# Scan of a gated delta rule on one core: the chunk's inverse as T(1+A)(1+A²), summed in PSUM

## The reference, cut to what matters

```python
def step(S, inp):
    w_t, k_t, v_t, kk_t, a_t = inp[:5]
    s_kk = jnp.einsum('nbhvk,nbhk->nbhv', S, kk_t)
    S = S * w_t[..., None, :] - s_kk[..., :, None] * (kk_t * a_t)[..., None, :] + v_t[..., :, None] * k_t[..., None, :]
    y_t = jnp.einsum('nbhvk,nbhk->nbhv', S, inp[5]) if emit else None
    return S, y_t
```

## Time and profile before

| | |
|---|---|
| runs | 5050.57, 5038.10, 5045.04 us; median 5045.04 |
| profiled execution | 5050.79 us, its span 5049.0 us |
| granted TensorE clock, mean over the span | 0.975 |
| PE matmul busy | 4816.4 us (95%), 27502 records |
| DVE, ACT, POOL busy | 1475.1, 1053.9, 321.6 us |
| the scan's steady rounds | from 3000.66 to 3421.77 us of the span |

### The profile page before, as it was taken

One profiled execution on the slowest core, in us unless ns is written; L12 is line 12 of the kernel. 1 busy time (PEld: TensorE's weight loads), 2 busy tenths in 40 slices (PEclk: granted clock), 3 DMA queues, 4 the chain that ended last, 5 costly groups with the idle time before them and its releaser, 6 DMA issues.

```text
span 5049.0 us, 63120 instructions
## 1 busy us (share of the span) xinstructions
PE 4816.4 (95%) x27502; PEld 2642.5 (52%) x27502; DVE 1475.1 (29%) x2777; ACT 1053.9 (21%) x2046; POOL 321.6 (6%) x302
## 2 busy tenths in 40 slices
PE   8999999999999999999998989998999999899999
PEld 4444444444444445665554568786444555544444
DVE  3621110462121010000324347775102444310100
ACT  1131000123100022110214124443112333311210
POOL 1100000110000000000014100000000010000000
PEclk9999999999999999999999999999999999899999
DMA  3151212125122211111134422223111000011211
GB/s 121 59 200 68 83 62 80 61 75 192 67 75 68 82 42 59 50 50 43 62 133 134 140 70 78 78 74 114 48 47 45 26 28 32 26 43 74 82 68 58
DMA packets 91841, 378.36 MB, mean 75 GB/s; under 512 B 7985, under 2 KB 33713, under 8 KB 62129
## 3 DMA queue, kind: packets, MB, share of 16 engines
q1 hardware_dynamic: 80608, 332.92, 18.7%
q0 software_dynamic: 9808, 37.75, 2.3%
q10 hardware_dynamic: 1152, 3.67, 0.2%
HBM read 334.46 MB, written 39.85 MB: 74 GB/s over the span
## 4 chain that ended last, share of the span: by engine, by line
PE 91%; DVE 4%; ACT 2%; issue 2%; DMA 0%; POOL 0%; POOLq 0%; SPq 0%; DVEq 0%; ACTq 0%
PE ps L521 43%; PE ps L333 23%; PE ps L542 7%; PE ps L3385 2%; PE ps L1781 2%; PE ps L339 1%; PE ps L3312 1%; PE ps L990 1%; PE ps L946 1%; PE ps L3396 1%; PE ps L2477 1%; PE ps L2428 1%; PE ps L3315 1%; PE ps L3311 1%; PE ps L3313 1%
## 5 line engine op out<-in xcount | busy, mean ns | idle before, releaser
L521 PE MATMUL ps<-A,W 128*128 128x512 f32 (+1 forms) x5408 | 2174.4, 562 | 24.5 <-DVE A L493 8.8
L521 PEld LDWEIGHTS ps<-A,W 128*128 128x128 f32 x5408 | 1028.5, 191 | 1118.9 <-issue 1076.0
L333 PE MATMUL ps<-A,W 64*64 64x64 f32 (+3 forms) x3264 | 664.5, 380 | 17.3 <-DMA W<-in_rw_in 6.1
L333 PEld LDWEIGHTS ps<-A,W 128*128 128x128 f32 (+2 forms) x3264 | 351.5, 162 | 309.7 <-issue 277.9
L333 PE MATMUL ps<-A 64*64 64x64 f32 (+3 forms) x8416 | 446.6, 238 | 63.3 <-ACT A L3538 23.2
L333 PEld LDWEIGHTS ps<-A 64*64 64x64 f32 (+2 forms) x8416 | 408.5, 148 | 166.7 <-issue 94.3
L542 PE MATMUL ps<-W,A 128*128 128x512 f32 (+1 forms) x896 | 367.6, 572 | 1.8 <-ACT A L1567 1.8
L542 PEld LDWEIGHTS ps<-W,A 128*128 128x128 f32 x896 | 173.1, 194 | 191.7 <-issue 183.6
L435 ACT ACTIVATE A<-R 128x512 f32<-128x512 f32 (+1 forms) x96 | 52.6, 574 | 782.7 <-DVE R L1577 354.6
L1697 DVE SCALAR_TENSOR_TENSOR A<-ps,V,A 128x512 f32<-128x512 f32 (+1 forms) x48 | 31.0, 661 | 486.9 <-PE ps L333 486.3
L1577 DVE SCALAR_TENSOR_TENSOR R<-ps,MOD,R 128x512 f32<-128x512 f32 (+1 forms) x48 | 31.7, 662 | 439.4 <-PE ps L521 438.1
(11 more groups left out here) (358 smaller groups left out, 4210.0 us busy)
## 6 DMA issues: line engine op xcount, KB each, us to landing
W<-in_ada SPq DMA_DIRECT2D x48, 1024.0 KB, 5.3
W<-in_w_up SPq DMA_DIRECT2D x44, 1024.0 KB, 4.8
W<-in_w_down SPq DMA_DIRECT2D x32, 704.0 KB, 4.0
W<-in_w_in SPq DMA_DIRECT2D x18, 1024.0 KB, 4.8
W<-in_sgu_v SPq DMA_DIRECT2D x16, 1024.0 KB, 4.9
W<-in_sgu_u SPq DMA_DIRECT2D x16, 1024.0 KB, 4.8
W<-in_sgu_z SPq DMA_DIRECT2D x16, 1024.0 KB, 4.9
W<-in_sgu_o SPq DMA_DIRECT2D x16, 1024.0 KB, 4.7
```

The costliest lines, as they stand in the source:

```text
L333: r = e.matmul(out, a, b, start=start and i == 0, stop=stop and i == len(pairs) - 1, skip_group_check=loose)
L521: t = e.matmul(ps, w[:, k, c:c + mc], x(k, seg), start=k == 0, stop=k == kt - 1)
```

## The change

The two rounds that add an identity give way to one square and one product that don't need each other. The first `series` makes A² = `nE`ᵀ`nEt` with no identity; the second makes T(1+A) (turned) from `Z1` and `T16`, also with no identity; ACT puts the first into `Z2` and the second over `nE`. `inverse` then sums 64 products in place of 32 into the same two banks: for each head T(1+A)·A² and T·(1+A). The number of banks taken, the order of the strands and the copies on ACT, DVE and POOL stay. DVE's wait before it overwrites `nE` moves from `Z3` to `Q` of the step before.

```diff
--- before.py
+++ after.py
@@ -2449,7 +2449,6 @@
 
     S_, b = pl.S, pl.scan
     AR, KA, KD, KB = b.AR[s % 3], b.KA[s % 2], b.KD[s % 2], b.KB[s % 2]
-    one = table(pl, "id64")
 
     def blocks(g):
         names = [(k, s, g, c) for k in ("Et", "E") for c in range(2)]
@@ -2472,27 +2471,26 @@
         e.wait_ge(*event)
         for x in names:
             e.wait_ge(*free(pl, x))
-        for c in range(2):
-            i = one[HALF[c], :].rearrange("p (o c) -> p o c", o=1).to_broadcast([64, 8, 64])
-            e.matmul(by_heads(ps[c][HALF[c], :]), one[HALF[c], :], i, start=True, stop=False, skip_group_check=True)
         for hh in range(8):
             for c in range(2):
                 t = product(e, ps[c][HALF[c], 64 * hh:64 * hh + 64],
-                            [(left[HALF[c], 8 * g + hh, :], right[HALF[c], 8 * g + hh, :])], start=False, loose=True)
+                            [(left[HALF[c], 8 * g + hh, :], right[HALF[c], 8 * g + hh, :])])
         t.then_inc(*S_.inverse_made.next((s, g, stage)))
 
     def inverse():
 
         names = [("Q", s, c) for c in range(2)]
         ps = [take(pl, x, "0123") for x in names]
-        e.wait_ge(*S_.act_blocks.at(s, 1, "Z3"))
+        e.wait_ge(*S_.act_blocks.at(s, 1, "TZ"))
         for x in names:
             e.wait_ge(*free(pl, x))
         for hh in range(8):
-            for g in range(2):
-                for c in range(2):
-                    t = product(e, ps[c][HALF[g], 64 * hh:64 * hh + 64],
-                                [(b.T16[HALF[c], 8 * g + hh, :], b.Z1[HALF[c], 8 * g + hh, :])])
+            for left, right in ((b.nE, b.Z2), (b.T16, b.Z1)):
+                for g in range(2):
+                    for c in range(2):
+                        t = product(e, ps[c][HALF[g], 64 * hh:64 * hh + 64],
+                                    [(left[HALF[c], 8 * g + hh, :], right[HALF[c], 8 * g + hh, :])],
+                                    start=hh == 0 and left is b.nE, stop=False, loose=True)
         t.then_inc(*S_.inverse_made.next((s, "Q")))
 
     def tokens(c):
@@ -2534,12 +2532,12 @@
     tokens(0)
     yield
     for g in range(2):
-        series(g, "Z2", b.nE, b.Z1, S_.pool_blocks.at(s, g))
+        series(g, "A2", b.nE, b.nEt, S_.dve_blocks.at(s, g, "E"))
         yield
     tokens(1)
     yield
     for g in range(2):
-        series(g, "Z3", b.nE, b.Z2, S_.act_blocks.at(s, g, "Z2"))
+        series(g, "TZ", b.Z1, b.T16, S_.pool_blocks.at(s, g))
         yield
     values(None)
     yield
@@ -2681,12 +2679,12 @@
     tokens(0)
     yield
     for g in range(2):
-        series(g, "Z2", b.Z2)
+        series(g, "A2", b.Z2)
         yield
     tokens(1)
     yield
     for g in range(2):
-        series(g, "Z3", b.Z1)
+        series(g, "TZ", b.nE)
         yield
     e.wait_ge(*S_.inverse_made.at(s, "Q"))
     if s >= 2:
@@ -2865,7 +2863,7 @@
     def blocks(g):
         e.wait_ge(*S_.inverse_made.at(s, g, "E"))
         if s and g == 0:
-            e.wait_ge(*S_.inverse_made.at(s - 1, 1, "Z3"))
+            e.wait_ge(*S_.inverse_made.at(s - 1, "Q"))
         for name, dst, mask in (("Et", b.nEt, later), ("E", b.nE, earlier)):
             for c in range(2):
                 at = (name, s, g, c)
```

## The result

| | before | changed |
|---|---|---|
| median of 20 runs each, us | 5050.31 (5038.10 to 5067.22) | 5037.47 (5023.59 to 5047.03) |
| ratio | | 0.9974, 95% interval 0.9966 to 0.9983 |
| profiled execution, span, us | 5049.0 | 5035.1 |
| scan, from the first decay product of its own to the first product of the output stage, us | 519.08 | 504.28 |
| nine steady rounds, us | 380.69 | 366.10 |

The change is faster by 0.26%, 13 us, with 9 to 17 inside the interval. 5037.47 lies in that range. The gain of 13 us lies between my own case (13 to 21, forecast 16.5) and the rival in which the supply takes more (10.5), and 0.26% falls into the outcome "within 0.3%", which I had given 0.41 against 0.54 for more.

What follows compares the result with a forecast made beforehand. Taken as bound: PE up to L, then DVE's chain. Ten rounds at 1.3 (13.0 us), 1.45 before the first and 2.0 in the last make 16.5 us: 5045.04 - 16.5 = 5028.5 us, range 5015 to 5041.

Steps and rivals of the forecast that it cites:

- my own case: Whole kernel: a gain of 13 to 21 us, time 5024 to 5032 us; chance 0.50.
- the rival in which the supply takes more: Quick stretch after L: at 3.7 us a packet a round gains 0.7, the sum 10.5 us, time 5034.5; chance 0.37.
- within 0.3%: Whole kernel: the outcome of a difference of at most about 15 us, not told from no change; chance 0.41.
- What bounds it: Scan rounds: PE sets the time up to L, then DVE's chain, 18.1 us from L's end to the next round.
- The removed identities: Z2 and Z3: 3.5 us of PE per step; 1.70 a round before L shortens it, 1.75 after L lies beside DVE.
- The added products: Q after L: 64 more records at 15 ns, 0.94 us per step, 11 us in all, hidden while PE ends before DVE.
- The moved waits: POOL's sum, Z2's copy, DVE's waits for Q, ACT's copies: the moved waits cost nothing.
- The supply of instructions: Second `series` product to next round: three packet intervals, 10.6 us, make PE late; net loss 0.3 a round, plus 0.1 in L.
- Ten rounds at 1.3: Scan: ten rounds gain 1.70 - 0.4 = 1.3 us each, 13.0 in sum.
- the slower rival: Second `series` product to round's start: packets at 4.5 us lose 1.85 a round, 15 us slower, 5060; chance 0.05.
- Before the first round, and the last: Scan's ends: 1.45 us off DVE's wait for L's copy before the first round, 2.0 us off the last.
- All of PE's saving: Whole kernel: PE bounds everywhere, so all 31 us land, time 5014; chance 0.08.

Runs made afterwards that it cites:

- the slow order of Q: The changed kernel with Q's products ordered by group, alternating two row halves of one column half, 29 ns a record in place of 15: 0.9983 of the kernel before.
- the second trace: The changed kernel profiled and timed once more with no edit, beside two others on one chip: 0.9975 of the kernel before.

## Why the prediction was right, and where not

**What bounds it.** Right: PE up to L, 22.52 us before and 20.8 after; 19.1 us from L to the next round in both, 19.5 in the other direction. Taking Z2's identities away gives their time, taking Z3's away gives none.

**The removed identities.** Right to a few hundredths: 1.70 per round on the path was forecast, 1.7 is what the stretch ahead of L lost.

**The added products.** The price was right. P, Y and Q made a row of 128 records in 3.18 us and make one of 192 in 4.1 now, 0.93 for 64. Neither the estimate of 25 ns by the Trainium skill ("TensorEngine Tiling (Array Packing)", Instruction Overhead) nor the 29 ns came true. In two quadrants it would not have mattered in a round: there the supply sets the pace.

**The moved waits.** Right: in the nine rounds no transpose of DVE waited for Q, and PE waited neither for POOL nor for the copy of A².

**The supply of instructions.** The mechanism is shown (the slow order of Q trades 13 us of waits for 14 of busy time at no cost; 1.14 a round when Q is doubled, part of it through DVE's chain), but the term was sized too high: 0.4 a round. From L to the next round, the rounds where PE was late lost 1.5 us in sum before, 1.9 in the first trace after, out of nine: 0.05 a round. Two more rounds of that trace reached L 0.8 and 0.6 us late, which did not come again in this size in the second trace. My reckoning let three whole packet intervals of 3.5 us follow one another; that PE had more in hand when the stretch began would explain the difference, but isn't shown. By size, "mostly hidden", as the Trainium skill has it ("Runtime: NRT & Kernel Launch", Instruction fetch mechanics), was nearer than my term; the stalls of 1.5 us show that it is not wholly so.

**Ten rounds at 1.3.** Nine rounds fell by 14.6 us (1.62 each), of which 2.4 are the stray stall of the trace before; 1.36 without it, 1.75 in the second trace. (My formula for the slower rival gives 1.4 at 3.5 us a packet where the sum has 1.3; nothing hangs on it.) Right in size, in part by luck: the supply took less than I gave it, and the first round of the first trace lay at a clock of 0.95 and gained nothing.

**Before the first round, and the last.** 1.45 was forecast ahead of the first; the traces show 1.29 and 0.0 (38.75 before, 37.46 and 38.78 after). For the last part 3.3 was forecast (one round of 1.3 and 2.0); it got 1.1 us longer, or 0.2 shorter in the second trace. This is the step that failed. "Both pairs of identities count, less the added products, less some stall" left out that the clock falls in this part, behind a wait of 3.03 us on DVE that both kernels have (0.98 before, 0.95 and 0.97 now), and put PE's supply too low there: its waits for "issue" rose from 0.7 us to 6.0 in the first trace and 4.5 in the second. From 3408.06 to 3425.00 the granted clock was 0.70. In these rows of the changed kernel `blocks(0)` takes 2.97 and `blocks(1)` 3.70 us:

```profile
3408.40 2.97 PE L333 MATMUL ps<-A 64*64 64x64 f32 x64
3414.41 3.70 PE L333 MATMUL ps<-A 64*64 64x64 f32 x64 [3.03 <-DVE A L2870]
3418.04 1.82 PE L333 MATMUL ps<-A,W 128*64 128x128 f32 x16
```

where the kernel before had 2.10, 3.62 and 1.09. As an estimate from the clocks, 6 us more at half speed cost up to 3 of the shortfall in the first trace, and the waits for "issue" 5.3; how much of either was hidden isn't shown. The sum of the scan: 16.5 forecast, 14.8 and 18.3 in the two traces; without the stray stall of the trace before, 12.4 and 15.9.

**The rivals.** All of PE's saving (31 us) did not land. The supply did not take more. The slower case did not come, nor was its mechanism the dangerous one: the doubled Q cost 1.14 a round, near the price of 1.1 that I had for a spent supply, and rounds did not grow from one to the next. The rival that was missing is the clock. Without the added work in Q the change had its idle time beside DVE turned into half clock at six of ten starts, as in the kernel without Z3's identities.

**Left open.** Why the clock drops at six of ten starts without Z3's identities and not at every one (a start behind 1.80 us was at full clock, one behind 0.89 at half); and what sets the distance of packets, 2.9 to 4.2 us.

## What to carry to other kernels

Ask first on which side of the hand-over between two engines the removed work stands: the same identities were worth 15 us ahead of L and minus 11 behind it. Where an engine idles beside another's chain, look at its granted clock before you count removed work as free, and do not add up measured parts that share one slack. When many short products follow one another, their pace may be worth nothing: Q at half its rate left the nine rounds as they were. Starting the other engine's chain earlier, with slow products moved between the quick ones, was worth 0.2 to 0.3% here; the move of the slow ones alone was inconclusive.

## What the runs showed of the hardware

- TensorE fell to half clock at six of ten starts of a round, behind waits for DVE of 0.9 to 2.0 us, and with 64 added records a step it stayed up: nine rounds of 389.9 us at a clock of 0.97 against 378.3 at 1.00. Less work was slower.
- PE runs out of instructions in quick stretches: 126 records at 15 ns would take 1.9 us, and a packet of them came every 2.9 to 4.2. PE went on 2.3 to 2.9 us after the transfer of a packet had started. At 29 ns a record the waits for issue fall from 15.8 to 2.6 us.
- A POOL product of 128x1024 float32 (2.36 us) held a DVE product of that shape beside it: 3.10 us in place of 1.23.
- Code that is the same in all kernels moved between traces: what stands ahead of the scan ended at 2955.7 to 2967.7 us, what follows it took 1554.9 to 1572.3. A difference of 10 us in the span says nothing of the scan unless its own stretch is read.
